# Hybrid encoder trunk on one core: the opening's weight tiles loaded and split by halves, one x block on another queue

## What is computed

```python
def swiglu_ffn(x, w_up, w_down):
    gate, up = jnp.split(x @ w_up, 2, axis=-1)
    return (jax.nn.silu(gate) * up) @ w_down

for l in range(DEPTH):
    x = layer_norm(ALPHA * x + 0.5 * swiglu_ffn(x, ffn1_w_up[l], ffn1_w_down[l]), ln1_g[l], ln1_b[l])
    ...
```

## Time and profile before

| what | us |
|---|---|
| median of 3 runs | 1103.27 |
| lowest and highest run | 1101.51, 1104.18 |
| the profiled execution, its own time | 1103.1 |
| its span, first to last instruction | 1101.2 |
| first product of the opening starts | 5.31 |
| first product of the second chunk starts | 17.59 |
| TensorE busy over the span | 1091.8 |

### The profile page before, as it was taken

How to read it: one execution, slowest core, us unless ns; L and a number is a source line. 1 busy time by engine, 2 the same in 40 slices (tenths; PEclk the granted TensorE clock), 3 DMA queues, 4 the chain that set the end, 5 groups by cost and what they waited for, 6 DMA issues and landing times.

```text
span 1101.2 us, 18278 instructions
## 1 busy us (share of the span) xinstructions
PE 1091.8 (99%) x6377; PEld 926.4 (84%) x6377; DVE 789.2 (72%) x1084; ACT 584.6 (53%) x839; POOL 372.6 (34%) x442
## 2 busy tenths in 40 slices
PE   9999999999999999999999999999999999999997
PEld 7888888998788888888888888889877888888886
DVE  6667777789877867775676666477898787666744
ACT  6655443574873555554345555336858645555540
POOL 2998974108600288992300000011284000000001
PEclk9999999999999999999999999999999999999999
DMA  8966774744576586677466666636545666666651
GB/s 283 293 189 189 253 229 131 221 128 136 159 228 192 170 273 191 190 227 231 137 205 193 189 208 207 226 89 214 168 131 155 206 197 215 193 185 206 208 183 39
DMA packets 159423, 211.09 MB, mean 192 GB/s; under 512 B 12952, under 2 KB 107384, under 8 KB 159360
## 3 DMA queue, kind: packets, MB, share of 16 engines
q1 hardware_dynamic: 155232, 202.29, 58.4%
q10 hardware_dynamic: 2688, 3.70, 1.3%
q0 software_dynamic: 1440, 4.27, 1.2%
HBM read 209.11 MB, written 1.10 MB: 191 GB/s over the span
## 4 chain that ended last, share of the span: by engine, by line
PE 94%; DVE 2%; issue 1%; DMA 1%; ACT 0%; SPq 0%; POOLq 0%; POOL 0%; DVEq 0%; ACTq 0%
PE ps L838 24%; PE ps L780 16%; PE ps L782 16%; PE ps L781 16%; PE ps L842 12%; PE ps L1160 2%; PE ps L1162 1%; PE ps L1163 1%; DVE wlo L1281 1%; DMA raw<-in_ffn_w_up 1%; PE ps L794 1%; PE ps L1028 1%; PE ps L1046 1%; PE ps L1075 1%; PE ps L1096 1%
## 5 line engine op out<-in xcount | busy, mean ns | idle before, releaser
L1281 DVE TENSOR_TENSOR wlo<-raw,whi 128x1024 fp32r<-128x1024 f32 (+1 forms) x371 | 480.5, 1318 | 197.8 <-ACT whi L447 195.0
L447 ACT CAST whi<-raw 128x1024 fp32r<-128x1024 f32 (+1 forms) x371 | 377.5, 1042 | 214.1 <-PE ps L782 124.0
L838 PE MATMUL ps<-x_hl,whi 128*128 128x512 f32 x1152 | 362.6, 396 | 0.0
L842 PEld LDWEIGHTS ps<-x_hl,wlo 128*128 128x128 f32 x1152 | 216.6, 188 | 50.9
L842 PE MATMUL ps<-x_hl,wlo 128*128 128x256 f32 x1152 | 226.6, 278 | 0.0
L1734 POOL TENSOR_TENSOR rstd<-var_eps,cst 128x1 f32<-128x1 f32 x12 | 18.3, 1528 | 533.9 <-DVE var_eps L1347 524.8
L838 PEld LDWEIGHTS ps<-x_hl,whi 128*128 128x128 f32 x1152 | 175.8, 189 | 0.3
L780 PE MATMUL ps<-whi,x_hl 128*128 128x512 f32 (+1 forms) x400 | 156.9, 392 | 0.1
L781 PE MATMUL ps<-wlo,x_hl 128*128 128x512 f32 (+1 forms) x400 | 153.2, 383 | 0.0
L782 PE MATMUL ps<-whi,x_hl 128*128 128x512 f32 (+1 forms) x400 | 153.2, 383 | 0.0
L780 PE MATMUL ps<-whi,hh 128*128 128x512 f32 (+1 forms) x355 | 138.2, 389 | 0.5 <-DVE hl L1332 0.5
(11 more groups left out here) (200 smaller groups left out, 1384.8 us busy)
## 6 DMA issues: line engine op xcount, KB each, us to landing
raw<-in_ffn_w_up SPq DMA_DIRECT2D x351, 256.0 KB, 3.6
raw<-in_ffn_w_down SPq DMA_DIRECT2D x176, 256.0 KB, 3.3
raw<-in_w_in SPq DMA_DIRECT2D x128, 256.0 KB, 3.5
raw<-in_w_branch SPq DMA_DIRECT2D x32, 256.0 KB, 3.2
raw<-in_w_out SPq DMA_DIRECT2D x32, 256.0 KB, 3.7
bias_g<-bias_rows ACTq DMA_DIRECT2D x16, 192.0 KB, 4.0
raw<-in_w_in SPq DMA_DIRECT2D x16, 148.0 KB, 2.2
affine<-in_ln_g SPq DMA_DIRECT2D x4, 512.0 KB, 6.2
```

Source lines behind the costliest of these rows:

```text
L447: nc.scalar.copy(whi[:, s % RING, 0:w], raw[:, s % RAW, 0:w]).then_inc(S["hi_done"], 1)
L838: nc.tensor.matmul(ps[:, bank, :], w(whi, s + q, at, at + P), x_hl[:, k, :, :], start=k == 0, stop=False)
L842: ins = nc.tensor.matmul(ps[:, bank, 0:SEQ], w(wlo, s + q, at, at + P), xh[:, k, :], start=False, stop=k == KT - 1)
L1281: nc.vector.tensor_tensor(wlo[:, s % RING, 0:w], raw[:, s % RAW, 0:w], f32(whi[:, s % RING, 0:w]), ALU.subtract).then_inc(S["split_done"], 1)
```

## The change

In the opening, tiles 1 to 3 are treated as tile 0 was: each is loaded in three transfers (its first half, 256 KB, then two pieces of 128 KB of its second half), rounded and split by halves, and TensorE waits for the halves one by one, in the same order of products for all four tiles. The x block of the second token tile, half 0, is no longer issued by ScalarE but by SP, behind tile 0; the orders of ScalarE and VectorE between tiles and x blocks stay. The number of warm-up products goes from nine to eight. Tiles 4 and later are treated as before. Semaphore declarations are left out here.

```diff
--- before.py
+++ after.py
...
@@ -365,23 +366,24 @@
             def load_columns(i, half):
                 sp.dma_start(x_cols[:, i, half, :], A["x_t"][i, half]).then_inc(xt_landed[2 * i + half], 16)
 
-            def load_first(w):
-                dst = raw[:, 0, :].rearrange("p (t g n) -> p t g n", t=2, g=2)
-                sp.dma_start(dst[:, 0], w[0, :, 0, :, 0, :]).then_inc(S["first_landed"], 16)
+            def load_halves(q, w):
+                dst = raw[:, q, :].rearrange("p (t g n) -> p t g n", t=2, g=2)
+                sp.dma_start(dst[:, 0], w[0, :, 2 * q, :, 0, :]).then_inc(half_landed[q], 16)
                 for g in range(2):
-                    sp.dma_start(dst[:, 1, g], w[0, :, 1, g, 0, :]).then_inc(raw_landed[0], 16)
+                    sp.dma_start(dst[:, 1, g], w[0, :, 2 * q + 1, g, 0, :]).then_inc(raw_landed[q], 16)
 
             def ffn(l, which, n, s0):
                 w_up = A[f"ffn{which}_w_up"].rearrange("l (t p) (g c n) -> l p t g c n", p=P, g=2, c=NC_UP)
                 w_dn = A[f"ffn{which}_w_down"].rearrange("l (k p) (h n) -> l k p h n", p=P, h=2)
                 for c in range(PEEL):
                     if n == 0 and c == 0:
-                        load_first(w_up)
-                        up_chunk(l, 0, s0, w_up, 0, range(1, 2))
+                        load_halves(0, w_up)
+                        load_columns(1, 0)
+                        load_halves(1, w_up)
                         load_columns(0, 1)
-                        up_chunk(l, 0, s0, w_up, 0, range(2, 3))
+                        load_halves(2, w_up)
                         load_columns(1, 1)
-                        up_chunk(l, 0, s0, w_up, 0, range(3, 4))
+                        load_halves(3, w_up)
                         sp.dma_start(ident[:, :], A["ident"]).then_inc(S["ident_landed"], 16)
                     else:
                         up_chunk(l, 0, s0 + 4 * c, w_up, c)
@@ -751,19 +753,22 @@
                 nc.scalar.copy(xh[:, 4 * half:4 * half + 4, tok(i)], x_cols_half(i, half)
                                ).then_inc(S["xh_done"], 1)
 
-            for i in range(NT):
-                act.dma_start(x_cols[:, i, 0, :], A["x_t"][i, 0]).then_inc(xt_landed[2 * i], 16)
+            def halves_hi(q):
+                act.wait_ge(half_landed[q], 16)
+                nc.scalar.copy(whi[:, q, 0:512], raw[:, q, 0:512]).then_inc(S["half_hi"], 1)
+                act.wait_ge(raw_landed[q], 32)
+                nc.scalar.copy(whi[:, q, 512:1024], raw[:, q, 512:1024]).then_inc(S["hi_done"], 1)
+
+            act.dma_start(x_cols[:, 0, 0, :], A["x_t"][0, 0]).then_inc(xt_landed[0], 16)
             columns_hi(0, 0)
-            act.wait_ge(S["first_landed"], 16)
-            nc.scalar.copy(whi[:, 0, 0:512], raw[:, 0, 0:512]).then_inc(S["first_hi"], 1)
-            act.wait_ge(raw_landed[0], 32)
-            nc.scalar.copy(whi[:, 0, 512:1024], raw[:, 0, 512:1024]).then_inc(S["hi_done"], 1)
+            halves_hi(0)
             columns_hi(1, 0)
-            splits(1, 1)
+            halves_hi(1)
             columns_hi(0, 1)
-            splits(2, 1)
+            halves_hi(2)
             columns_hi(1, 1)
-            splits(3, 5)
+            halves_hi(3)
+            splits(4, 4)
             for l in range(DEPTH):
                 ffn(2 * l, first(l), 0 if l == 0 else None)
                 transition(3 * l + 1, mix(l, MIX0), l)
@@ -852,42 +857,30 @@
                     return nc.tensor.matmul(ps[:, t, :], a[:, k, tok(t)], w(ring, q, at, at + 512),
                                             start=start, stop=stop)
 
-                pe.wait_ge(S["xh_done"], part(0, 0, 0))
-                pe.wait_ge(S["first_hi"], 1)
-                product(xh, whi, 0, 0, 0, start=True)
-                pe.wait_ge(S["x_ready"], part(0, 0, 0))
-                product(xl, whi, 0, 0, 0)
-                pe.wait_ge(S["first_lo"], 1)
-                product(xh, wlo, 0, 0, 0)
-                pe.wait_ge(S["hi_done"], 1)
-                product(xh, whi, 0, 1, 0)
-                product(xl, whi, 0, 1, 0)
-                wait_split(0)
-                product(xh, wlo, 0, 1, 0)
-                pe.wait_ge(S["xh_done"], part(0, 1, 0))
-                for k in range(2):
-                    product(xh, whi, 0, k, 1, start=k == 0)
-                    product(xh, wlo, 0, k, 1)
-                pe.wait_ge(S["x_ready"], part(0, 1, 0))
-                for k in range(2):
-                    ins = product(xl, whi, 0, k, 1)
-                ins.then_inc(S["pe_used"], 1)
-                for q in range(1, 4):
-                    for t in range(NT):
-                        pe.wait_ge(S["x_ready"], part(0, t, q // 2))
-                        if t == 0:
-                            pe.wait_ge(S["hi_done"], q + 1)
-                        for k in (2 * q, 2 * q + 1):
-                            for a in (xh, xl):
-                                product(a, whi, q, k, t)
-                        if t == 0:
-                            wait_split(q)
-                        for k in (2 * q, 2 * q + 1):
-                            ins = product(xh, wlo, q, k, t, stop=k == KT - 1)
-                        if t == 1:
-                            ins.then_inc(S["pe_used"], 1)
-                        elif q == 3:
-                            ins.then_inc(S["up_done"], 1)
+                for q in range(4):
+                    k, k2 = 2 * q, 2 * q + 1
+                    pe.wait_ge(S["xh_done"], part(0, 0, q // 2))
+                    pe.wait_ge(S["half_hi"], q + 1)
+                    product(xh, whi, q, k, 0, start=q == 0)
+                    pe.wait_ge(S["x_ready"], part(0, 0, q // 2))
+                    product(xl, whi, q, k, 0)
+                    pe.wait_ge(S["hi_done"], q + 1)
+                    product(xh, whi, q, k2, 0)
+                    product(xl, whi, q, k2, 0)
+                    pe.wait_ge(S["half_lo"], q + 1)
+                    product(xh, wlo, q, k, 0)
+                    wait_split(q)
+                    ins = product(xh, wlo, q, k2, 0, stop=q == 3)
+                    if q == 3:
+                        ins.then_inc(S["up_done"], 1)
+                    pe.wait_ge(S["xh_done"], part(0, 1, q // 2))
+                    product(xh, whi, q, k, 1, start=q == 0)
+                    product(xh, whi, q, k2, 1)
+                    product(xh, wlo, q, k, 1)
+                    product(xh, wlo, q, k2, 1)
+                    pe.wait_ge(S["x_ready"], part(0, 1, q // 2))
+                    product(xl, whi, q, k, 1)
+                    product(xl, whi, q, k2, 1, stop=q == 3).then_inc(S["pe_used"], 1)
                 pe.wait_ge(S["ident_landed"], 16)
                 up_pass(4, 1, 0)
                 up_pass(4, 1, 1)
@@ -1253,7 +1246,7 @@
                     nc.tensor.matmul(ps[:, 2, 0:P], k0_t[:, 0, :], k0_t[:, 1, :], start=True, stop=True)
 
             pe.wait_ge(S["const_ready"], 1)
-            warm_up(9)
+            warm_up(8)
             for l in range(DEPTH):
                 ffn(2 * l, 3 * l, first(l), 3 * l + 1, 0 if l == 0 else None)
                 mixer(l)
@@ -1672,19 +1665,23 @@
                 nc.vector.tensor_tensor(xl[:, k, tok(i)], x_cols_half(i, half), f32(xh[:, k, tok(i)]), ALU.subtract
                                         ).then_inc(S["x_ready"], 1)
 
+            def halves_lo(q):
+                dve.wait_ge(S["half_hi"], q + 1)
+                nc.vector.tensor_tensor(wlo[:, q, 0:512], raw[:, q, 0:512], f32(whi[:, q, 0:512]), ALU.subtract
+                                        ).then_inc(S["half_lo"], 1)
+                dve.wait_ge(S["hi_done"], q + 1)
+                nc.vector.tensor_tensor(wlo[:, q, 512:1024], raw[:, q, 512:1024], f32(whi[:, q, 512:1024]), ALU.subtract
+                                        ).then_inc(S["split_done"], 1)
+
             columns_lo(0, 0)
-            dve.wait_ge(S["first_hi"], 1)
-            nc.vector.tensor_tensor(wlo[:, 0, 0:512], raw[:, 0, 0:512], f32(whi[:, 0, 0:512]), ALU.subtract
-                                    ).then_inc(S["first_lo"], 1)
-            dve.wait_ge(S["hi_done"], 1)
-            nc.vector.tensor_tensor(wlo[:, 0, 512:1024], raw[:, 0, 512:1024], f32(whi[:, 0, 512:1024]), ALU.subtract
-                                    ).then_inc(S["split_done"], 1)
+            halves_lo(0)
             columns_lo(1, 0)
-            splits(1, 1)
+            halves_lo(1)
             columns_lo(0, 1)
-            splits(2, 1)
+            halves_lo(2)
             columns_lo(1, 1)
-            splits(3, 5)
+            halves_lo(3)
+            splits(4, 4)
             for l in range(DEPTH):
                 ffn(2 * l, first(l), 0 if l == 0 else None)
                 transition(3 * l, mix(l, MIX0), affine)
```

More of the change, by code:

```diff
@@ L216, in build @@
     xt_landed = [sem(f"xt_landed{i}") for i in range(2 * NT)]
+    half_landed = [sem(f"half_landed{i}") for i in range(RAW)]
     x_landed = [sem(f"x_landed{i}") for i in range(NT)]
```

(2 more changed lines are left out.)

## The result

The changed kernel took 1104.51 us in the median (22 runs, 1102.53 to 1109.48), the kernel before on the same chip 1102.62 (22 runs, 1101.44 to 1104.63): ratio 1.0016, interval [1.0009, 1.0023]. The forecast was 0.7 us less, with a range up to 1104.5. The kernel became 1.9 us slower instead, just outside the range. That is less than the 3.3 us that the prediction took as the least that can be told from no change, yet with 22 runs of each the interval lies wholly above 1. The profiled execution of after took 1105.81 for a span of 1104.0, 1.3 above its own median; the one of before took 1103.1, 0.5 above its median of these runs. So the two profiles differ by 2.8 us of span, more than the medians, and I use them for places, not for the size.

A forecast was written before the change was run, and what follows sets the result against it. TensorE was taken as busy 99% of the span, so only the opening's waits, at best about 1.7 us, could be won; tile 7's earlier split gave 0.7 us off, 1102.6 us from 1103.27, range 1100.9 to 1104.5.

The forecast's parts named there:

- Bytes and their order are the same, so I leave the landings where they were: Opening, tiles 1 to 3: transfers land as before, tile 1 at 7.46 us and tile 3 at 12.64.
- ScalarE loses one issue: Opening, ScalarE's queue: one transfer issue fewer, 0.45 us, at a time when ScalarE would wait for x anyway.
- the backlog: DMA queues at 7.47 us: 1.37 MB still unmoved, lasting until 11.3 us and covering SP's later issues by 0.2 to 0.9.
- After that TensorE has no wait for weights that would swallow it: After tile 7: the 0.7 us gained in the opening is kept to the end.
- The first half tile: Start of the opening: first weight half lands at 4.0 us, first product near 4.9, 0.4 us earlier.
- Tile 0's second half: Opening: lands at 5.2 us in place of 5.94; the products of tile 0 end at 8.1.
- Tiles 1 to 3: Opening: halves ready 1.31 us after landing against 2.28; TensorE need not wait from 8.1, first chunk ends at 16.25 us.
- Tile 4 and tile 7: Second chunk: tile 4 lands at 14.6 us again, tile 7 at 18.5 to 19.0, split near 21.2 against 21.92.
- The predicted wait for tile 4: Start of the second chunk: TensorE is free at 16.25 us and waits 0.7 us for tile 4's split.
- SP's queue: Opening: four more issues on SP, reaching tile 4 at 9.6 to 10.2 us in place of 7.47; no cost taken.
- SP comes too late: Rival, chance 0.15, at tile 4's issue: tile 4 lands 2.1 to 2.7 us later, time 1104.2 to 1104.9 us.
- The lower clock: Rival, chance 0.15: TensorE stays slow in the opening, 0.45 us a product; only 0.2 us off, 1102.9 us.

The follow-up runs named there:

- p4: Kernel before with only the x block of the second token tile issued by SP behind tile 0; ratio 1.0018 [1.0006, 1.0029].
- p2: Changed kernel with the x block of the second token tile back on ScalarE's queue; ratio 0.9995 [0.9984, 1.0005].
- f2: Kernel before with the x block on SP and a GpSimd pause late in the second layer's preparation; 1103.07 us, ratio 0.9999.
- e2: Kernel before with eight warm-up products in place of nine; ratio 0.9991 [0.9975, 1.0007].
- p1: Kernel before with three more semaphores that nobody uses; ratio 1.0011 [1.0000, 1.0022].
- f1: Kernel before with a GpSimd pause late in the second layer's preparation, until VectorE's last hl is written; 1102.33 us, ratio 0.9991.
- e1: Changed kernel with nine warm-up products in place of eight; ratio 1.0008 [0.9995, 1.0020].
- e3: Changed kernel with two products of zeros added after TensorE's second product of tile 0; 1104.62 us, ratio 1.0018 [1.0002, 1.0034].
- e4: Changed kernel with the low part of a tile's first half multiplied before its second half's high part; 1104.19 us, ratio 1.0008.
- p3: Changed kernel with two transfers per opening tile in place of three; ratio 1.0018 [1.0006, 1.0029].
- f3: Changed kernel with a GpSimd pause late in the second layer's preparation; 1102.82 us, ratio 1.0000 [0.9989, 1.0012].
- f4: Changed kernel with the x block back on ScalarE's queue and a GpSimd pause late in the second layer's preparation; 1101.99 us, ratio 0.9992.
- g1: Changed kernel with the GpSimd pause and the x block of the first token tile's second half added to ScalarE's queue; 1103.23 us, ratio 0.9987.
- g2: Changed kernel with the GpSimd pause and three x blocks on ScalarE's queue; ratio 1.0017 [1.0006, 1.0028].
- t1: Kernel before with the second layer left out, yardstick of the one-layer kernels; 559.20 us.

## Why the prediction was wrong

**The step that failed** is "Bytes and their order are the same, so I leave the landings where they were", with the sentence that ScalarE loses one issue. I had priced the moved x block as an issue of 0.52 us on SP, hidden by the backlog, and at nothing for the stream. The backlog was there; the rate was not. 0.2 MB less was moved by 8 us (1.81 against 2.01). Alone the move costs 1.0018 [1.0006, 1.0029] (p4), and taking it back makes the changed kernel level with before (p2). In the old opening the way from the block to the time shows: p4 and f2 start the third chunk at 29.73, the four profiles with the block on ScalarE's queue (before, e2, p1, f1) at 27.89 to 28.89. Where the working weighed the Trainium skill, "DMA: Bandwidth & Descriptors", section "Issuing engines are not separate DMA queues", by which several issuing engines save only sequencer time, I objected to the size of that time and kept the rest of the rule. The runs speak against the rest: the issues were in time, and the bytes were slower.

**A second step failed, after the opening.** "After that TensorE has no wait for weights that would swallow it" holds for weights, and missed hl. The waits of the weight loads in before had a row for it that I did not weigh:

```profile
PEld ps L780 <- DVE hl L1332: 0.7, 1, 0.7
```

In after it is 2.4 us, 1.6 of it near 487 us. My view of the chain ended at 33 us. In the changed kernel this counts for more than the opening: where its loads are fast early, it starts the third chunk at 28.37 to 28.61 (e1, e3, e4, p3, f3), ahead of before's 28.89 and within 0.25 us of f4, which has the block on ScalarE's queue. What the profiles of e1, e3, e4 and p3 lose against that of before, they lose behind that point. How the place of the x block makes these later waits longer is not shown.

**The first half tile.** Nearly right. Predicted to land at 4.0, with a first product at 4.9; rounded at 4.38, right behind x, with a first product at 5.15. In the eight profiles with one block on ScalarE's queue it is rounded at 4.18 to 4.38, in the others at 4.48 to 5.16. The block that had left did hasten it. It did not hasten x of the first token tile, cast at 3.67 here in place of 3.52.

**Tile 0's second half.** Predicted to land at 5.2, taking 0.26 MB off at 360 GB/s; rounded at 5.74 here, and at 5.3 to 6.4 in the other profiles of this opening (e1, e3, e4, p3, f3). In after the fall of the rate, 4.2 to 4.8 us, lies before its landing.

**Tiles 1 to 3.** Tile 3's last half was predicted to land at 12.64 and is rounded from 13.04, 0.4 us late, but nothing waited for it: TensorE was later still.

**Tile 4 and tile 7.** Right on weights: 14.70 for 14.6, and 19.07 for a landing of 18.5 to 19.0. The predicted wait for tile 4 did not appear, because TensorE reached the second chunk at 18.74 in this execution and not at 16.25. In f3, the same opening, it was 17.46.

**SP's queue.** Right: 9.62 for 9.6, and no fall of the rate from 8 to 16 us, 280 GB/s and more in every slice. The rival "SP comes too late" had its place wrong: the rate falls at 4 to 5 us, not at tile 4's issue.

**The lower clock.** Its rival's picture came true in the profile of after, 0.43 us a product until about 10. It does not come from the moved block: p2, with the block back, shows the same and is level with before in the median, while f3, with the block on SP, has fast loads soon after its first. Whether the change as a whole makes a late rise likelier is open: loads of 330 ns last until about 10 us or longer in four of the ten two-layer profiles of the changed opening (after, p2, g1, g2) and in none of the six of the old one. The working that I drew from the mean clock of 0.998, 2.2 us of cycles missing in the warm-up, was wrong: the column reads 1.00 there, and the missing cycles lie in the last 11 us. Its conclusion, that the clock rose at the warm-up's very end, was right by luck: before's loads take 333 ns up to 4.84 us and 187 from 5.28 on.

**What the loss is made of.** Pooled over the runs without the pause (82 with x on SP; 163 with it on ScalarE's queue, most of them of the kernel before), the medians differ by 1.5 us, resampled interval 1.1 to 1.9; with the pause (24 and 24) by 0.6, interval 0.3 to 1.3. So some 0.6 us of the move's price is there without the wait near 487 us. Whether the rest is that wait, which more of the profiles with x on SP show (3 of 6 against 1 of 4), is suggested but not shown: the two intervals overlap. Why one queue alone moves less just between 4.2 and 5.8 us, and 280 to 400 GB/s from 8 us on, is open too. The fall comes 1 to 2 us after ScalarE's queue has run empty: the last packet there ends at 3.1 to 3.3 us with one block, at 4.5 to 4.8 with two. In p2, with two, a smaller fall, to 195, comes at 6.6 us.

## What to carry to other kernels

Before moving a transfer from one issuing queue to another, look at the DMA rate in the stretch where the second queue would run empty, and try the move alone: the bytes are the same, the rate need not be. An opening that wins a microsecond can be drowned by later stages whose length depends on the phase of two engines; compare the stretches from the opening to the end in several profiles before believing either. Extra traffic on the second queue can also cost: in g2 it pushed back the bytes that TensorE needed first.

## What the runs showed of the hardware

- The slowest slice of 0.2 us between 4.2 and 5.8 us moved 77 to 210 GB/s in the eight two-layer kernels with one x block on ScalarE's queue, and 251 to 374 in the seven with two there (g1 among them). By 8 us the first had moved 1.72 to 1.90 MB, the second 1.94 to 2.13.
- VectorE's split of 128x1024 takes 1.23 us alone and 2.04 to 2.15 in the splits shown that start inside a GpSimd operation on 128x512. With GpSimd's last operations moved by 22 us, the stretch with the wait near 487 us took 359.2 to 359.4 us in all six profiles, against 359.1 to 361.3 without.
- A wait of TensorE of 1.85 us, up to 491.69 us, was followed by a lower granted clock in the profile of e2 (PE busy and count, clock, DMA share, GB/s); after the wait of 2.13 us in t1 products came 0.43 us apart, the pace of the 1.2 GHz level. Waits of 1.3 to 1.4 us (after, e3, p1, g2) were not followed by it.

```profile
480.00:490.00 10.00, 9.84 (x57) 1.00 0.53 167
490.00:500.00 10.00, 8.31 (x29) 0.83 0.55 163
```

- The time at which loads go from 331 to 188 ns in the opening lay between 4 and 14 us in these profiles, and differed between executions of one and the same opening (after and f3).
